# Gated scan: keys and queries grown level by level from block decays, in place of running sums and exponentials

## What is computed

```python
def chunked_gated_scan(q, k, v, log_g):
    """S_t = diag(exp(log_g_t)) S_{t-1} + k_t^T v_t ; o_t = q_t S_t"""
...
def bidir_scan(q, k_f, k_b, v, lg_f, lg_b):
    flip = lambda t: jnp.flip(t, axis=2)
    o_f = chunked_gated_scan(q, k_f, v, lg_f)
    o_b = flip(chunked_gated_scan(flip(q), flip(k_b), flip(v), flip(lg_b)))
    return o_f + o_b
```

## Time and profile before

| | before |
|---|---|
| median of 3 runs | 3813.46 us |
| lowest and highest | 3802.16 and 3821.61 us |
| the profiled execution, its own time | 3804.65 us |
| its span in the profile | 3802.8 us |
| first scan stage (layer 0), with Modulate | 568.9 to 850.6 us of the span |
| second scan stage (layer 1), with Bias | 1582.0 to 1870.0 us |
| PE, DVE, ACT, GpSimd busy, share of the span | 82, 56, 35 and 15% |

### The profile page before, as it was taken

One profiled execution on the slowest core, in us unless ns is written; L12 is line 12 of the kernel. 1 busy time (PEld: TensorE's weight loads), 2 busy tenths in 40 slices (PEclk: granted clock), 3 DMA queues, 4 the chain that ended last, 5 costly groups with the idle time before them and its releaser, 6 DMA issues. The chain is left out here.

```text
span 3802.8 us, 83247 instructions
## 1 busy us (share of the span) xinstructions
PE 3134.4 (82%) x36396; PEld 2654.8 (70%) x36396; DVE 2142.7 (56%) x3567; ACT 1341.1 (35%) x2390; POOL 578.6 (15%) x466
## 2 busy tenths in 40 slices
PE   7999986666899999645468998779999688886699
PEld 7988884444798888534357897777778577775344
DVE  3455447877625555479776365466676344553452
ACT  3133325644421333356443232234444122221541
POOL 0200004431002000145310011001000122221100
PEclk9999996767999999856589999899999699998899
DMA  3532213214435221131243344463331421112330
GB/s 126 173 98 79 79 39 97 79 48 164 151 101 184 80 79 47 55 74 48 81 163 127 138 153 146 160 187 112 110 103 61 116 48 40 45 40 70 144 108 34
DMA packets 268263, 378.79 MB, mean 100 GB/s; under 512 B 45173, under 2 KB 207277, under 8 KB 266552
## 3 DMA queue, kind: packets, MB, share of 16 engines
q1 hardware_dynamic: 165834, 260.49, 22.2%
q10 hardware_dynamic: 102066, 112.97, 8.6%
HBM read 256.42 MB, written 118.94 MB: 99 GB/s over the span
## 5 line engine op out<-in xcount | busy, mean ns | idle before, releaser
L385 PE MATMUL psum<-proj_w_low,h_high 128*128 128x344 f32 (+1 forms) x1984 | 668.9, 337 | 17.5 <-DVE proj_y L411 14.4
L385 PE MATMUL psum<-proj_w_high,h_high 128*128 128x344 f32 (+1 forms) x1984 | 658.0, 332 | 0.0
L385 PE MATMUL psum<-proj_w_high,h_low 128*128 128x344 f32 (+1 forms) x1984 | 657.1, 331 | 0.0
L385 PEld LDWEIGHTS psum<-proj_w_low,h_high 128*128 128x128 f32 x1984 | 376.8, 190 | 33.4 <-DVE proj_y L411 16.2
L385 PEld LDWEIGHTS psum<-proj_w_high,h_high 128*128 128x128 f32 x1984 | 376.7, 190 | 6.9
L385 PEld LDWEIGHTS psum<-proj_w_high,h_low 128*128 128x128 f32 x1984 | 376.3, 190 | 7.1
L385 PE MATMUL psum<-proj_rest_w_low,h_high 128*128 128x304 f32 x640 | 207.7, 325 | 34.2 <-DVE proj_rest_w_low L400 22.6
L869 POOL TENSOR_TENSOR scan_d<-scan_b 128x384 f32<-128x384 f32 x112 | 124.2, 1109 | 622.5 <-DVE scan_b L710 608.6
L411 DVE COPY proj_y<-psum 128x344 f32<-128x344 f32 (+1 forms) x130 | 70.3, 541 | 243.7 <-PE psum L385 235.2
L1169 DVE COPY diff_wt<-psum 128x512 f32<-128x512 f32 x64 | 44.3, 692 | 282.6 <-PE psum L1115 282.6
L385 PE MATMUL psum<-proj_rest_w_high,h_low 128*128 128x304 f32 x640 | 194.6, 304 | 0.0
(11 more groups left out here) (416 smaller groups left out, 6954.7 us busy)
## 6 DMA issues: line engine op xcount, KB each, us to landing
proj_raw<-in_w_in SPq DMA_DIRECT2D x24, 1376.0 KB, 6.6
proj<-proj_y ACTq DMA_DIRECT2D x192, 172.0 KB, 1.8
delta_x<-dn_qkv SPq DMA_DIRECT2D x40, 384.0 KB, 5.2
proj<-proj_y ACTq DMA_DIRECT2D x68, 224.0 KB, 1.9
dn_prep_x<-proj SPq DMA_DIRECT2D x54, 256.0 KB
proj_raw<-in_w_in SPq DMA_DIRECT2D x7, 1792.0 KB, 9.3
modulate_w<-in_mod_w SPq DMA_DIRECT2D x16, 768.0 KB, 4.6
merge_z<-proj SPq DMA_DIRECT2D x8, 1536.0 KB, 7.2
```

The source lines that it names most:

```text
L385: last = PE.matmul(self.ps[:, j % self.banks, 0:self.width], hp[:, kt, tokens], wp[:, c % 2, kt, :], start=kt == 0 and n == 0, stop=kt == ...
```

## The change

The decays are no longer taken from running sums of logarithms. The gate itself is written to `decay[0]`, for both directions and three channel groups. At each level DVE multiplies neighbouring blocks' decays to the decays of blocks of twice the length (`decay[l]`; the last one is the tile's `gt`). The keys (`kts`) and queries (`qd`) are multiplied in place, half of them at each level, by the decay of the neighbouring block. Ahead of that, ACT copies the half that the level's scores need into `mks` and `mqs` ("packs"). So the running sums, GpSimd's differences, the logarithms of the second branch's gates, the exponentials of each level and `kd` are gone. `Scan` has no GpSimd program any more.

The order is also a new one. `PERIOD` is 24, and every part of `attend(n)` has a number of its own tile: first scores 14.15, scores of the first branch 20.4, last scores 21, placings 15.7, 21.6 and 23.6, `am` 23.2 and 24.9, product with the values 26.5, copy of `o` 27.3. The load of tile n stands at (n-2)·24 + 27.5.

```diff
--- before.py
+++ after.py
@@ -490,20 +490,21 @@
     VCOL = ((256, 256, 0), (1312, P, 256), (1440, P, 384))
     GLA_LEVELS, HGRN_LEVELS = 6, 7
-    SPACES = 4
-    PERIOD = 28
+    PERIOD = 24
+    FIRST, LEVEL = 9.4, 1.45
...
+        self.decay = [t(f"decay{l}", [P, 2, 3, P >> l]) for l in range(LEVELS)]
+        self.z, self.e, self.sg, self.f1 = t("z", [P, 512]), t("e", [P, 2, 512]), t("sg", [P, 2, 512]), t("f1", [P, 256])
...
@@ -533,7 +534,7 @@
             SP.dma_start(self.lbt[:, 3:4], bc(a["c_layers"][layer:layer + 1, 0:1], [P, 1])).then_inc(*c.inc())
             SP.dma_start(self.lbl[:].rearrange("p l t -> p (l t)"), a["hgrn_lb_logits"].rearrange("l (t p) -> p (l t)", p=P)).then_inc(*c.inc())
         for n in range(NT):
-            yield (n - 2) * self.PERIOD + 56 if n >= 2 else 0
+            yield (n - 2) * self.PERIOD + 27.5 if n >= 2 else 0
             nat, loaded = self.nats[:, n % 2], self.nat[n % 2]
             rows = self.p1[n * P:(n + 1) * P]
             if n >= 2:
...
@@ -546,9 +547,9 @@
 
         yield from by_time(*(paced(program(n), n * self.PERIOD, 1) for n in range(NT) for program in (attend, prepare)))
 
-    def space(self, n, l):
-
-        return self.d[:, (LEVELS * n + l - 1) % self.SPACES]
+    def at_level(self, l):
+
+        return self.FIRST + self.LEVEL * (l - 1)
 
     def pe(self):
         self.nc.tensor.wait_ge(*self.consts(8))
...
@@ -576,15 +577,15 @@
         for j, col in enumerate((0, 544, 672, 128)):
             last = PE.transpose(ps[:, 6, j * P:j * P + P], nat[:, col:col + P], ident[:])
         last.then_inc(*self.qk_turned.inc())
-        yield 18.5
-        PE.wait_ge(*self.faded(n))
+        yield 20
+        PE.wait_ge(*self.keys_grown(LEVELS * n + LEVELS - 1))
         if self.modulate is not None:
             PE.wait_ge(*self.modulate.added(2 * n + 1))
         for r in range(2):
             for j in range(3):
-                last = PE.transpose(ps[:, 6 + r, j * P:j * P + P], self.kd[:, r, j, :], ident[:])
+                last = PE.transpose(ps[:, 6 + r, j * P:j * P + P], self.kts[:, r, j, :], ident[:])
         last.then_inc(*self.keys.inc())
-        yield 21
+        yield 21.8
         PE.wait_ge(*self.kn_copied(n))
         for r in range(2):
             for j, (col, w, at) in enumerate(self.VCOL):
...
@@ -613,15 +614,18 @@
                         last = PE.matmul(ps[key:key + 64, 4 + r, col:col + 64], mk[rows, l, 1 + q, key:key + 64], queries(l)[rows, 1 + q, query:query + 64],
                                          start=True, stop=True, tile_position=(64 * r, key))
             return last
-        yield 24
-        PE.wait_ge(*self.mixed(8 * n + 3))
+        yield self.at_level(4) + 0.4
+        PE.wait_ge(*self.diagonal(n))
+        PE.wait_ge(*self.keys_packed(LEVELS * n + 2))
+        PE.wait_ge(*self.queries_packed(LEVELS * n + 2))
         if n:
             PE.wait_ge(*self.made64(n - 1))
         for l in range(4):
             last = scores64(l, l, False)
         last.then_inc(*self.scored.inc())
-        yield self.PERIOD + 5.5
-        PE.wait_ge(*self.mixed(8 * n + 7))
+        yield 20.4
+        PE.wait_ge(*self.keys_packed(LEVELS * n + LEVELS - 1))
+        PE.wait_ge(*self.queries_packed(LEVELS * n + LEVELS - 1))
         if n:
             PE.wait_ge(*self.o_copied(n - 1))
         for l in range(6):
...
@@ -635,12 +639,12 @@
             for h in range(4):
                 last = score32(7, h, key, 64 - key, 64, 192 + 64 - key)
         last.then_inc(*self.scored.inc())
-        yield self.PERIOD + 10.6
+        yield 21
         PE.wait_ge(*self.placed(3 * n))
         for l in range(4, 8):
             last = scores64(l, l - 4, l == 7)
         last.then_inc(*self.scored.inc())
-        yield self.PERIOD + 23.5
+        yield 26.5
         PE.wait_ge(*self.made32(n))
         PE.wait_ge(*self.made64(n))
         for h in range(8):
...
@@ -685,52 +687,56 @@
         V.scalar_tensor_tensor(out=e[:, 1, :], in0=ps[:, 7, :], scalar=0.0, in1=z[:], op0=ALU.max, op1=ALU.add).then_inc(*self.signs.inc())
         yield 5
         V.wait_ge(*self.log_a(n))
...
+        V.scalar_tensor_tensor(out=lt[:], in0=lt[:], scalar=0.0, in1=two(f1[:]), op0=ALU.min, op1=ALU.subtract).then_inc(*self.log_sig.inc())
         yield 6.2
         V.wait_ge(*self.sig_f(n))
         for j in range(2):
...
+            m = vo.mark(V.tensor_scalar(decay[0][:, :, 1 + j, :], self.by_channels(sg[:, 0], j), self.oml[:, j:j + 1], self.lb[:, j:j + 1], ALU.mult, ALU.add))
+        V.wait_ge(*self.sig_k(n))
+        if n:
+            V.wait_ge(*self.keys(n - 1))
+        for j in range(2):
+            keyed = V.tensor_scalar(kt[:, :, 1 + j, :], self.by_channels(sg[:, 1], j), self.oml[:, j:j + 1], None, ALU.mult)
+        keyed.then_inc(*self.keyed.inc())
         V.wait_ge(*m)
...
+        floored = vo.mark(V.tensor_scalar(decay[0][:, :, 1:3, :], decay[0][:, :, 1:3, :], 1e-30, None, ALU.max))
+        yield 8
+        V.wait_ge(*self.keyed(n))
         V.wait_ge(*self.qk_copied(n))
         if n:
             V.wait_ge(*self.scored(3 * (n - 1) + 1))
...
+        V.tensor_tensor(mk[:, 0], kt[:, 0], kt[:, 1], ALU.add).then_inc(*self.diagonal.inc())
+        V.wait_ge(*floored)
+        V.wait_ge(*self.decay_a(n))
+        V.tensor_tensor(queries, bc(qt.unsqueeze(1), [P, 2, 3, P]), decay[0][:], ALU.mult).then_inc(*self.begun.inc())
         for l in range(1, LEVELS + 1):
...
+            yield self.at_level(l) + 0.8
+            half, blocks = 1 << l - 1, P >> l - 1
+            total = decay[l - 1][:].rearrange("p r j b -> p (r j b)")
+            more = decay[l][:].rearrange("p r j b -> p (r j b)") if l < LEVELS else self.gt[:, n].rearrange("p r j -> p (r j)")
+            if l > 1:
+                V.wait_ge(*m)
+            else:
+                V.wait_ge(*self.begun(n))
+            if n:
+                V.wait_ge(*self.queries_grown(LEVELS * (n - 1) + min(l, LEVELS - 1)))
+            m = vo.mark(V.tensor_tensor(more, total[:, 0::2], total[:, 1::2], ALU.mult))
+            V.wait_ge(*self.keys_packed(LEVELS * n + l - 1))
+            keys = self.sides(kt[:, 0], l, 0, 3 * P + half, 1)
+            V.tensor_tensor(keys, keys, self.totals(total, l, 1, 3 * blocks - 1), ALU.mult).then_inc(*self.keys_grown.inc())
+            V.wait_ge(*self.queries_packed(LEVELS * n + l - 1))
+            later = self.sides(queries[:, 0], l, 3 * P, half - 3 * P, 1)
+            V.tensor_tensor(later, later, self.totals(total, l, 3 * blocks + 1, -3 * blocks - 1), ALU.mult).then_inc(*self.queries_grown.inc())
+        yield 22.6
+        V.wait_ge(*self.updated(n))
+        V.tensor_tensor(self.u[:, n, 0], ps[:, 6, :], self.heads[:], ALU.mult)
+        V.tensor_tensor(self.u[:, n, 1], ps[:, 7, :], self.heads[:], ALU.mult).then_inc(*self.fed.inc())
+
+    @staticmethod
+    def totals(x, l, first, side):
+
+        half = 1 << l - 1
+        return bass.AP(tensor=x.tensor, offset=x.offset + first, ap=[x.ap[0], [2, 3 * P // (2 * half)], [side, 2], [0, half]])
 
     @staticmethod
     def sides(x, l, first, side, step):
...
@@ -750,21 +756,21 @@
             near, mask = self.near64[:].rearrange("p (q r) t -> p r q t", r=2), bc(self.mask64[:, l].unsqueeze(1).unsqueeze(1), [P, 2, 2, 64])
             sc = ps[:, 4:6, l % 4 * 128:l % 4 * 128 + 128].rearrange("p r (q t) -> p r q t", q=2)
             return V.copy_predicated(near, mask.bitcast(U32), sc) if l else V.tensor_tensor(near, sc, mask, ALU.mult)
-        yield self.PERIOD + 7.7
+        yield self.at_level(5) + 0.5
         V.wait_ge(*self.scored(3 * n))
         for l in range(4):
             placed = place64(l)
             if l < 3:
                 vo.chain(placed)
         placed.then_inc(*self.placed.inc())
-        yield self.PERIOD + 14.9
+        yield 21.6
         V.wait_ge(*self.scored(3 * n + 1))
         for l in range(self.GLA_LEVELS):
             placed = place32(l)
             if l < self.GLA_LEVELS - 1:
                 vo.chain(placed)
         placed.then_inc(*self.placed.inc())
-        yield self.PERIOD + 18.3
+        yield 23.6
         V.wait_ge(*self.scored(3 * n + 2))
         V.wait_ge(*self.placed(3 * n))
         for l in range(4, self.HGRN_LEVELS):
...
@@ -792,59 +798,57 @@
         S.activation(z[:], z[:], ACT.Ln, bias=1.0).then_inc(*self.log_z.inc())
         yield 3.4
         S.wait_ge(*self.biased(n))
...
+        c(S.activation(f1[:], self.lt[:].rearrange("p j t -> p (j t)"), ACT.Abs))
+        c(S.activation(f1[:], f1[:], ACT.Exp, scale=-1.0))
+        S.activation(f1[:], f1[:], ACT.Ln, bias=1.0).then_inc(*self.log_a.inc())
         yield 4.9
         S.wait_ge(*self.signs(n))
         S.activation(sg[:, 0, :], e[:, 0, :], ACT.Exp).then_inc(*self.sig_f.inc())
         S.activation(sg[:, 1, :], e[:, 1, :], ACT.Exp, scale=-1.0).then_inc(*self.sig_k.inc())
+        yield 5.6
+        S.wait_ge(*self.log_sig(n))
+        if n:
+            S.wait_ge(*self.queries_grown(LEVELS * (n - 1)))
```

(58 more changed lines are left out.)

77 lines of the change are left out of this document (6 added, 71 removed).

## The result

The changed kernel took 3899.62 us in the median of 4 runs (3895.89 to 3901.03), the kernel before 3813.23 in 4 runs. The ratio is 1.0235, with a 95% interval from 1.0208 to 1.0262: slower by some 86 us. The profiled execution took 3895.89 (span 3894.1), so the two profiled executions are 91.2 apart.

What follows compares the result with a forecast made beforehand. The prediction took a full DVE plus a late load as the bound before, a ring across engines after. Layer 1's 19.3, Bias's 4 and layer 0's 36.2 made 59.5 us more than 3804.65: 3864, range 3790 to 3908.

Steps and rivals of the forecast that it cites:

- one ring: Scan stages: attending in its own tile puts scores, placings and products in series with DVE and ACT; chance 0.66.
- Bias's block: Layer 1, tile 2: Bias's GpSimd additions run in one block and slow DVE's levels, 4 us within 0 to 10.
- the first half: Layer 1 tile, PE's first turn until the queries are begun: 14.0 us.
- The second half: Layer 1 tile, from the level products through scores, turned keys and values to the copies of `u`: 22.9 us.
- the levels to the third copies: Second half's start, level products until the third level's copies, which PE's first scores need: 3.2 us.
- my 36.9: Time of a layer 1 tile after the first, once round the ring, in us.
- Modulate's second product: Layer 0, on PE between turning the queries and the first scores: 2.76 us.
- PE's clock: Rival, scan stages: PE at its upper clock everywhere saves 5.1 us a tile, 85 in all, giving 3779; chance 0.14.
- DVE stays the bound: Rival, scan stages: waits fall elsewhere, a stage takes 225 us instead of 300, giving 3714; chance 0.06.
- Levels twice as dear: Rival, DVE's level products and ACT's copies: a level takes 2.0 us, 5.6 more a tile, giving 3954; chance 0.10.
- The load stays late: Rival, tile loads: a load lands over 30 us after issue, adding nothing to the ring before that; no separate chance.
- nobody in the kernel before waited for the late scores: Kernel before: scores of tile n-1 ran while DVE and ACT worked on tile n, without delaying anyone; no size given.

Runs made afterwards that it cites:

- The square: Four kernels, old or new arithmetic, attending a tile later (3813, 3835.47 us) or in its own tile (3998.95, 3899.62 us).
- the kernel with three keys moved: Changed kernel with attended product, last copies into `am` and copy of `o` behind the next tile's projections: 3822.01 us, ratio 1.0027 to the kernel before.
- the other order: Changed kernel with scores one tile later, attended product two, more buffers, Modulate's products moved up, Bias's additions spread: 3740.16 us, ratio 0.9787 to the kernel before.
- the two kernels with the scores twice: First branch's scores of levels 0 to 5 made twice, in the changed kernel (3981.57 us) and in the kernel before (3859.55 us).

## Why the prediction was right, and where it was off

**The cause** was named: attention in its own tile turns parallel work into one ring, and DVE's savings fall into waits. The square and the kernel with three keys moved show it, and the expected signs stand in the profile: turns 36.3 to 39.0 us apart in layer 1 (I had said 36 to 38) but for the first, 31.4, and the one with Bias's block, 50.3, each ended by a copy of `u`; no wait for a load behind the first; the logarithm behind the copy of `o`; DVE's products at 0.55 and its share at 53%. The time, 3899.62, lies in the range, 36 above the forecast and 8 below the range's edge. What was mis-sized was nearly all too small, so little of this is errors that cancel, but the rise of 86 us is well above the 51 that 3864 gave.

**The sum, by its terms.** In the tile of the timeline above, the first half (first turn to the begun queries, 1829.43 to 1842.91) took 13.5 where I had 14.0. The second half took 24.3 where I had 22.9: the levels to the third copies 4.2 and not 3.2, since level 1 with its steps of two takes 0.85 and 0.87 for a product and 0.70 for a copy, the values 3.32 and not 3.0. The first tile took 31.4, as predicted, the last 43.8 against 44.2. What was mis-sized:
- *Bias's block*, where I took 4 us within 0 to 10: the tile took 13.4 more than my 36.9. The step that failed is the price, and with it the place: I scaled DVE's level products by the 1.20 to 0.54 of the earlier trace rows. But what fell beside the additions were the gates, the keys and their sum, and six instructions in a row took about one addition each, 13.7 us where they take 2.1 in the tile above. GpSimd's differences of a level were 1.1 to 1.2 us long in the median, the additions are 2.24. (The `lt` just ahead of the six took only 0.68, so one whole addition is not the price of each.) The Trainium skill (SBUF — State Buffer, "two separate sides") calls the port pair that the two share an exclusive lock, held for the full instruction, not a split of bandwidth; this trace agrees in the six, at 2.25 to 2.55 each beside additions of 2.24.
- *The other five tiles of layer 1*: 0.9 us each more than 36.9, 4.7 together. With 9.4 for Bias's tile (13.4 less the 4 I had put there) and 0.4 less in the last one, 13.7 in layer 1.
- *Modulate's second product*, which I had as 2.76, from a tile where PE came out of other work. In the new order it stands alone behind a wait, and takes 2.76 to 5.28, 11.3 us more than 2.76 over the eight tiles. A tile of layer 0 in the timeline of PE:

```profile
770.27 0.38 PE L565 MATMUL psum<-ident,scan_nats 128*16 128x128 f32 x2 [1.47 <-DVE u L733]
...
779.14 4.68 PE L1552 MATMUL psum<-modulate_w,modulate_ct 128*2 128x192 f32 x16
786.12 4.44 PE L1552 MATMUL psum<-modulate_w,modulate_ct 128*2 128x192 f32 x16 [2.31 <-DVE modulate_m L1524]
...
802.81 1.41 PE L614 MATMUL psum<-scan_mqs,scan_mks 64*64 64x64 f32 x64
...
808.99 0.38 PE L565 MATMUL psum<-ident,scan_nats 128*16 128x128 f32 x2 [1.47 <-DVE u L733]
```

The middle tiles of layer 0 took 38.0 to 39.6 and one 42.4, where I had 37.8: with the first and the last tile, 12.0 us in that stage. The product doesn't explain it tile by tile: the tile from 730.69 has it at 2.76 and yet takes 39.6, with two gaps (1.95 and 0.75) in its scores and 3.78 for the values.
- *Outside the stages* 6.0 us more in the profiled execution. What lies behind layer 1's scan took 1932 to 1952 us in the eleven profiles, with the same code in each; 6 us is within that, so I don't put it down to the change.

12.0 + 13.7 + 6.0 = 31.7, the distance between the profiled execution and the 3864 that was reckoned against one.

**The rivals.** (1) *PE's clock* did not decide: the granted clock fell to 0.67 and 0.55, and one matmul of the attended product took 421 ns in the median, against 275 before. That is the 3.67 of a tile, near the value I took. The last scores took 1.99 behind 240 small matmuls in the tile of layer 1 and 1.41 in the one of layer 0, so the lower level can hold behind that much small work, and does not always. The better clock came with the other order (1.90 for the product, 0.82 and 0.62 in the windows of the two stages). The 85 us that I gave this rival should have been 82, 16 times its 5.1. (2) *DVE stays the bound*: no, 53% in a tile. (3) *Levels twice as dear*: no; level 1 alone is 1.5 times a plain level. (4) *The load stays late*: no, in no tile.

**Wrong in the argument**, though it moved no number: that nobody in the kernel before waited for the late scores. They had slack, but less than 5 us: in layer 1 the sum of the keys comes to wait for them, in layer 0 Modulate's product behind them.

## What to carry to other kernels

When an engine's work shrinks and the time does not, look at whose results wait for whom around one round of the loop, and not at the busy shares: in layer 1's tile no engine was busy for more than 53%. Here it paid to put work that reads a tile's results one or two tiles behind it, with a copy of each buffer that it reads for that distance; moved a tile later with single buffers, it only traded one wait for another. A change of arithmetic and one of order made at the same time need four kernels to be told apart; here three sort keys held nine tenths of the loss.

## What the runs showed of the hardware

- A DVE instruction beside GpSimd may take as long as GpSimd's instruction: 0.37 us of work took 2.25 beside additions of 2.24. It matters when a GpSimd block runs, and how long one of its instructions is.
- PE stops in the middle of long groups of small matmuls, mostly for 0.6 to 2.7 us, ended by no engine ("issue"). In the two kernels with the scores twice these stops are nearly always 125 to 128 matmuls apart, or about 380. With the scores twice, the gaps in the first branch's scores came to 42.3 and 42.9 us in the two stages, against 12.7 and 10.3 in the kernel after. One of those gaps was 7.6 us long. By these sums (42.3 + 42.9 - 12.7 - 10.3) / 16 = 3.9 of the 5.2 us that the doubled scores cost a tile are such gaps. Where PE is on the chain, such a group costs more than its matmuls' own time.
- The view of the DMA queues counts as many packets of one instruction queue as PE has blocks of 256 instructions: in layer 1's scan 26 in the kernel after (3328 matmuls and as many weight loads), 38 with the scores twice (4864 and as many). 128 small matmuls with their weight loads are one such block. So the stops fit a wait for the next block; that is inferred, not tested.
- Once each in layer 1 of four kernels such a gap was 7.6 to 8.6 us, each time begun within 6 us of the issue of Bias's read back, while the DMA engines were 75% busy or more.
